# Eight groups of small steps set later in a one-core two-layer GDN and latent-attention kernel

## The reference, cut to what matters

```python
u = rms_norm(x, pre_mix)
qkv_a, z_a, a_a, b_a, cq, ckv, k_rope, gate_logits = split(u @ w_in)
qkv_a = silu(causal_conv(qkv_a, conv_w))          # width 4
q_a, k_a = l2_norm(q_a), l2_norm(k_a)             # per head of 128
g_a = -exp(A_log) * softplus(a_a + dt_bias); beta = sigmoid(b_a)
o_a = rms_norm(gated_delta_rule(q_a, k_a, v_a, g_a, beta)) * silu(z_a)
y_a = o_a @ w_branch_a
y_b = latent_attention(cq, ckv, k_rope) @ w_branch_b
x = x + rms_norm((sigmoid(g0) * y_a + sigmoid(g1) * y_b) @ w_out)
x = x + rms_norm(relu(rms_norm(x) @ w_ff1)**2 @ w_ff2)
```

## Time and profile before

| what | value |
|---|---|
| median of three runs | 1168.86 us (1162.62 to 1173.67) |
| the profiled execution | 1171.58 us |
| its span | 1169.8 us |
| TensorE matmuls busy | 1069.1 us, 91% |
| VectorE, ScalarE, GpSimd busy | 750.7, 568.7, 171.6 us |
| mean granted TensorE clock | 0.954 of full |

### The profile page before, as it was taken

One profiled execution on the slowest core, in us unless ns is written; L12 is line 12 of the kernel. 1 busy time (PEld: TensorE's weight loads), 2 busy tenths in 40 slices (PEclk: granted clock), 3 DMA queues, 4 the chain that ended last, 5 costly groups with the idle time before them and its releaser, 6 DMA issues.

```text
span 1169.8 us, 24158 instructions
## 1 busy us (share of the span) xinstructions
PE 1069.1 (91%) x10568; PEld 1033.3 (88%) x10568; DVE 750.7 (64%) x967; ACT 568.7 (49%) x789; POOL 171.6 (15%) x133
## 2 busy tenths in 40 slices
PE   6899878899999899999978988698899998999996
PEld 5888868789999899999878988697799997999996
DVE  6885526667757587744477845365786666886453
ACT  5565353663554444433356643545546444544431
POOL 7131000140000232200011300001400002221000
PEclk9989979998999899999979889799999998999999
DMA  7333322442455366566433433223423652665651
GB/s 256 106 121 105 115 70 90 125 132 88 145 179 182 108 185 194 169 207 184 144 108 108 145 97 107 69 94 110 145 88 129 216 185 88 217 185 191 185 182 49
DMA packets 45607, 163.84 MB, mean 140 GB/s; under 512 B 5184, under 2 KB 5440, under 8 KB 45504
## 3 DMA queue, kind: packets, MB, share of 16 engines
q1 hardware_dynamic: 44928, 161.50, 43.9%
q10 hardware_dynamic: 576, 0.81, 0.2%
HBM read 161.24 MB, written 1.05 MB: 139 GB/s over the span
## 4 chain that ended last, share of the span: by engine, by line
PE 76%; DVE 12%; ACT 6%; issue 4%; DMA 1%; SPq 0%; POOL 0%; POOLq 0%; DVEq 0%; ACTq 0%
PE dense L524 21%; PE dense L526 21%; PE dense L525 21%; DVE wlo L1235 4%; ACT whi L934 2%; DVE kT L1321 1%; PE sides L880 1%; PE sides L881 1%; DVE qT L1321 1%; PE sides L754 1%; PE sides L762 1%; DVE vT L1321 1%; PE sides L906 1%; ACT rn L945 1%; PE sides L916 1%
## 5 line engine op out<-in xcount | busy, mean ns | idle before, releaser
L1235 DVE TENSOR_TENSOR wlo<-raw,whi 128x1024 fp32r<-128x1024 f32 (+1 forms) x304 | 402.3, 1335 | 228.1 <-ACT whi L934 227.5
L934 ACT ACTIVATE whi<-raw 128x1024 fp32r<-128x1024 f32 (+1 forms) x304 | 314.1, 1046 | 216.9 <-PE dense L526 206.2
L524 PE MATMUL dense<-uh,whi 128*128 128x256 f32 x768 | 232.0, 302 | 3.4 <-DVE wlo L1235 2.0
L526 PE MATMUL dense<-uh,wlo 128*128 128x256 f32 x768 | 221.1, 288 | 2.7 <-issue 2.7
L525 PE MATMUL dense<-ul,whi 128*128 128x256 f32 x768 | 221.2, 288 | 1.1 <-issue 1.1
L524 PEld LDWEIGHTS dense<-uh,whi 128*128 128x128 f32 x768 | 151.8, 198 | 11.5 <-issue 7.6
L524 PE MATMUL dense<-fuh,whi 128*128 128x256 f32 x512 | 145.9, 285 | 9.8 <-DVE ful L1545 9.6
L525 PEld LDWEIGHTS dense<-ul,whi 128*128 128x128 f32 x768 | 151.7, 198 | 1.8 <-issue 1.4
L526 PEld LDWEIGHTS dense<-uh,wlo 128*128 128x128 f32 x768 | 151.4, 197 | 1.2 <-issue 1.2
L526 PE MATMUL dense<-fuh,wlo 128*128 128x256 f32 x512 | 145.2, 284 | 0.0
L525 PE MATMUL dense<-ful,whi 128*128 128x256 f32 x512 | 144.8, 283 | 0.0
(11 more groups left out here) (280 smaller groups left out, 2021.5 us busy)
## 6 DMA issues: line engine op xcount, KB each, us to landing
raw<-weights SPq DMA_DIRECT2D x304, 512.0 KB, 3.7
xT<-x_t SPq DMA_DIRECT2D x4, 256.0 KB, 4.4
out_t<-xT SPq DMA_DIRECT2D x4, 256.0 KB, 2.3
cst<-consts ACTq DMA_DIRECT2D x1, 512.0 KB, 7.0
prm_all<-params ACTq DMA_DIRECT2D x1, 150.0 KB, 3.9
pos_i<-pos ACTq DMA_DIRECT2D x1, 128.0 KB, 4.4
cst<-consts ACTq DMA_DIRECT2D x1, 2.0 KB, 4.8
```

Source lines behind the costliest of these rows:

```text
L524: mm(o_, h_[:, ws], ahi[:, k0 + k, :], start=is_first, stop=False, skip_group_check=True)
L526: x_ = mm(o_, l_[:, ws], ahi[:, k0 + k, :], start=False, stop=is_last, skip_group_check=True)
L934: return A(o_, i_, ACT.Copy)
L1235: TT(wlo[s][:, 0:w], raw[s][:, 0:w], f32(whi[s][:, 0:w]), ALU.subtract).then_inc(lo_ready, 1)
```

## The change

`schedule()` is rewritten between job `lat` 2 and job `uq` 0. Arithmetic, job order and weights are the same.

- `logits` becomes three steps: 0 behind job `k` 0 (PE's products and the first two operations of each of ScalarE and VectorE), 1 behind half `k` 1, 2 behind job `k` 1.
- All of `k` 1 to 3 and `z` 0 get halves; `gc` stands behind half `k` 2, `dt` 0 and 1 behind half `k` 3, `silu` n one half job later than before, `nrm`, `kk`, `dexp`, `ktrans`, `eg` spread over the halves of `z` 0 to 2; job `z` 3 is whole and stands ahead of `lvP` 0.
- `nrm` is split in `nsq` (GpSimd's squares, PE's sums) and `nrm` (ScalarE, VectorE), the second one later.
- The sixteen steps of the inverse and the state stand one each ahead of the sixteen halves of `v` and `q`; `vtrans` 0 to 3 behind job `v` 3, half `q` 0, half `q` 1 and job `q` 1; `silu` n of v and q one half job later.
- `kk` and `qk` go pair by pair of heads in the order 0, 2, 1, 3, so the first two need heads 0 to 3 only; `t_o` half 0 moves ahead of job `vt` 3, with the `side` banks swapped.
- The sign of `sinT` (GpSimd) becomes a step in the list behind `dt` 3.
- Layer 1 has the same three early splits as layer 0.
- SyncE issues the first quarter of x, then the first weight piece, then the other three quarters.

```diff
-    o += [("logits", 0), ("latn", 1)]
+    o.append(("latn", 1))
     job("k", 0)
-    o.append(("conv", 0))
+    o += [("logits", 0), ("conv", 0)]
+    half("k", 1)
+    o.append(("logits", 1))
     job("k", 1)
-    o += [("conv", 1), ("gc", 0), ("silu", 0), ("trig", 0), ("silu", 1)]
+    o += [("logits", 2), ("conv", 1)]
+    half("k", 2)
+    o += [("gc", 0), ("silu", 0), ("trig", 0)]
     job("k", 2)
-    o += [("conv", 2), ("dt", 0), ("dt", 1), ("silu", 2)]
+    o += [("silu", 1), ("conv", 2)]
+    half("k", 3)
+    o += [("dt", 0), ("dt", 1)]
     job("k", 3)
-    o += [("conv", 3), ("dt", 2), ("dt", 3), ("kr", 0), ("silu", 3), ("lnexp", 0)]
+    o += [("silu", 2), ("conv", 3), ("dt", 2), ("dt", 3), ("sign", 0), ("kr", 0)]
+    half("z", 0)
+    o += [("silu", 3), ("lnexp", 0), ("nsq", 0), ("nsq", 1), ("nrm", 0), ("nrm", 1)]
     job("z", 0)
...
+    between = [(kind, part, i) for kind in "vq" for i in range(4) for part in (half, job)]
+    behind = {n: [] for n in range(len(between) + 3)}
+    for n in range(8):
+        behind[2 * n + 2].append(("conv", 4 + n))
+        behind[2 * n + 3].append(("silu", 4 + n))
+    behind[0] += [("zsilu", i) for i in range(4)]
+    for n, at_ in enumerate((7, 8, 10, 11)):
+        behind[at_].append(("vtrans", n))
+    behind[15].append(("nsq", 4))
+    steps = [[(step, lv)] for lv in range(len(SIZES)) for step in ("lvP", "lvV")]
+    steps += [[(step, 0)] for step in ("pairP", "pairV", "lastP", "lastV")]
+    steps += [[(step, 0), (step, 1)] for step in ("t_v0", "t_st", "t_ks", "t_v1")]
+    for n, (kind, part, i) in enumerate(between):
+        o.extend(steps[n])
+        part(kind, i)
+        o.extend(behind[n])
+    half("gate", 0)
+    o += behind[16] + [("nsq", 5)]
     job("gate", 0)
-    o += [("lnexp", 1), ("nrm", 4), ("nrm", 5)]
+    o += behind[17] + [("lnexp", 1), ("nrm", 4), ("nrm", 5)]
     job("kn", 0)
+    o.append(("nsq", 6))
     job("kn", 1)
+    o.append(("nsq", 7))
+    job("kn", 2)
     o += [("nrm", 6), ("nrm", 7)]
-    job("kn", 2)
     job("kn", 3)
...
-            return {("xsplit", 1): 1, ("sq", 0): 2, ("sqsum", 1): 3}.get((what, n), 0) if l == 0 else 0
+            return l * NPIECE + {("xsplit", 1): 1 + l, ("sq", 0): 2 + l, ("sqsum", 1): 3 + l}.get((what, n), 0)
...
+            x_part(0)
             for n in range(DEPTH * NPIECE):
                 sp.wait_ge(lo_ready, n + 1)
                 sp.dma_start(raw[n % RING][:], w_in[n]).then_inc(loaded[n % RING], 16)
+                if n == 0:
+                    for c in range(1, 4):
+                        x_part(c)
```

More of the change, by code:

```diff
@@ L39 @@
 QUAD = 32
+PAIRS = [0, 2, 1, 3]
 KK_BANK = [4, 1, 3, 4]
+QK_BANK = [0, 2, 0, 2]
 SIZES = [2, 4, 8, 16]
@@ L138, in schedule @@
     job("z", 1)
-    o += [("kk", 0), ("kk", 1), ("dexp", 2), ("dexp", 3), ("eg", 0), ("eg", 1)]
+    o += [("kk", 2), ("ktrans", 0), ("eg", 0), ("eg", 1)]
     half("z", 2)
-    o += [("kk", 2), ("kk", 3), ("ktrans", 0), ("ktrans", 1), ("zero", 0)]
+    o += [("kk", 3), ("ktrans", 1), ("zero", 0)]
     job("z", 2)
     o.append(("x1", 0))
[L144 to L173, removed]
@@ L174, in schedule @@
-    for _ in fill:
-        pass
+    job("z", 3)
+    between = [(kind, part, i) for kind in "vq" for i in range(4) for part in (half, job)]
[8 more added lines that the diff above has]
+    steps = [[(step, lv)] for lv in range(len(SIZES)) for step in ("lvP", "lvV")]
@@ L187, in schedule @@
     job("vt", 2)
+    o.append(("t_o", 0))
     job("vt", 3)
-    o += [("t_o", 0), ("t_o", 1)]
+    o.append(("t_o", 1))
     for i in range(6):
@@ L480, in _, with x_part @@
         def _(sp):
-            for c in range(4):
+            def x_part(c):
                 sp.dma_start(xT[:, 2 * c:2 * c + 2, :], x_in[:, 2 * c:2 * c + 2, :]).then_inc(s_x[c], 16)
+            x_part(0)
             for n in range(DEPTH * NPIECE):
@@ L630, in norm, with logits @@
                 r.then_inc(sumsq, 1)
-            def logits(l, _):
+            def logits(l, part):
+                if part:
+                    return
                 pe.wait_ge(dve_evac, l * NDVE_EVAC + evacs_through(JOB["lat", 2])[1])
@@ L702, in ktrans @@
             def ktrans(l, half):
+                pe.wait_ge(nrm_out, due(l, nrm_out, 2 + 2 * half))
                 pe.wait_ge(kk_out, due(l, kk_out, 2 + half))
@@ L840, in t_o @@
             def t_o(l, half):
-                pe.wait_ge(qk_out, due(l, qk_out, 4))
-                pe.wait_ge(qd_out, due(l, qd_out, 2))
+                pe.wait_ge(qk_out, due(l, qk_out, 2 + 2 * half))
+                pe.wait_ge(qd_out, due(l, qd_out, half + 1))
+                if half == 0:
+                    pe.wait_ge(nrm_r, due(l, nrm_r, 15))
                 for e in range(4):
@@ L846, in t_o @@
                     cols = slice(e * P, (e + 1) * P)
-                    mm(side[half][:, cols], vn0[:, h, :], AT[:, half, e, :], start=True, stop=True)
-                    mm(side[2 + half][:, cols], st[:, h, :], qd[:, h, :], start=True, stop=False)
-                    r = mm(side[2 + half][:, cols], vn1[:, h, :], AT[:, 2 + half, e, :], start=False, stop=True)
+                    mm(side[1 - half][:, cols], vn0[:, h, :], AT[:, half, e, :], start=True, stop=True)
+                    mm(side[3 - half][:, cols], st[:, h, :], qd[:, h, :], start=True, stop=False)
+                    r = mm(side[3 - half][:, cols], vn1[:, h, :], AT[:, 2 + half, e, :], start=False, stop=True)
                 r.then_inc(t_om, 1)
@@ L918, in ysum @@
                 r.then_inc(y_mm, 1)
-            do = dict(norm=norm, logits=logits, dt=dt, job=job, gc=gc, vtrans=vtrans, nrm=nrm, latn=latn, kr=kr_, ktrans=ktrans, kk=kk, qk=qk,
+            do = dict(norm=norm, logits=logits, dt=dt, job=job, gc=gc, vtrans=vtrans, nsq=nsq, latn=latn, kr=kr_, ktrans=ktrans, kk=kk, qk=qk,
                       lvP=lvP, lvV=lvV, pairP=pairP, pairV=pairV, lastP=lastP, lastV=lastV, half=half, t_v0=t_v0, t_st=t_st, t_ks=t_ks, t_v1=t_v1, t_o=t_o, onrm=onrm,
@@ L999, in fsplit_x, with logits @@
                       scale=prm_all[:, l, PRE_FFN + c:PRE_FFN + c + 1]).then_inc(fu_hi, 1)
[L1001 to L1010, removed]
+            def logits(l, part):
+                if part == 0:
+                    act.wait_ge(ab_z, due(l, ab_z, 2))
+                    A(sm[:, 1, :], sm[:, 0, :], ACT.Abs).then_inc(ab_abs, 1)
+                    act.wait_ge(ab_abs, due(l, ab_abs, 1))
+                    A(sm[:, 2, :], sm[:, 1, :], ACT.Exp, scale=-1.0).then_inc(ab_ex, 1)
+                elif part == 1:
+                    act.wait_ge(ab_w, due(l, ab_w, 1))
+                    A(sm[:, 4, :], sm[:, 3, :], ACT.Ln).then_inc(ab_ln, 1)
+                else:
+                    act.wait_ge(ab_sp, due(l, ab_sp, 3))
+                    A(sm[:, 8, :].rearrange("p (t n) -> p t n", t=NT)[:, :, 8:16],
+                      sm[:, 7, :].rearrange("p (t n) -> p t n", t=NT)[:, :, 8:16], ACT.Exp, scale=-1.0).then_inc(ab_a, 1)
             def job(l, j):
@@ L1152, in t_o @@
                 act.wait_ge(t_om, due(l, t_om, half + 1))
-                copy(oT[:, hs, 0:P], side[half][:])
-                copy(oT[:, hs, P:2 * P], side[2 + half][:]).then_inc(t_oo, 1)
+                copy(oT[:, hs, 0:P], side[1 - half][:])
+                copy(oT[:, hs, P:2 * P], side[3 - half][:]).then_inc(t_oo, 1)
             def onrm(l, i):
@@ new lines, in logits @@
+                if part == 0:
+                    dve.wait_ge(ab_mm, due(l, ab_mm, 1))
+                    raw_ = side[2][:, 0:32].rearrange("p (t n) -> p t n", t=NT)
+                    TT(by_t(0)[:, :, 0:8], raw_[:, :, 0:8], over_t(prm_all[:, l, DTB:DTB + H]), ALU.add).then_inc(ab_z, 1)
+                    TS(by_t(0)[:, :, 8:16], raw_[:, :, 8:16], -1.0, None, ALU.mult).then_inc(ab_z, 1)
+                elif part == 1:
+                    dve.wait_ge(ab_ex, due(l, ab_ex, 1))
+                    TS(sm[:, 3, :], sm[:, 2, :], 1.0, None, ALU.add).then_inc(ab_w, 1)
+                    dve.wait_ge(ab_w, due(l, ab_w, 1))
+                    STT(sm[:, 5, :], sm[:, 3, :], -1.0, sm[:, 2, :], ALU.add, ALU.subtract).then_inc(ab_w, 1)
+                    V.reciprocal(sm[:, 6, :], sm[:, 3, :]).then_inc(ab_rc, 1)
+                    dve.wait_ge(ab_w, due(l, ab_w, 2))
+                    dve.wait_ge(ab_rc, due(l, ab_rc, 1))
+                    TT(sm[:, 5, :], sm[:, 5, :], sm[:, 6, :], ALU.mult).then_inc(ab_sp, 1)
+                else:
+                    dve.wait_ge(ab_sp, due(l, ab_sp, 1))
+                    dve.wait_ge(ab_ln, due(l, ab_ln, 1))
+                    TT(sm[:, 7, :], sm[:, 4, :], sm[:, 5, :], ALU.subtract).then_inc(ab_sp, 1)
+                    dve.wait_ge(ab_sp, due(l, ab_sp, 2))
+                    STT(sm[:, 7, :], sm[:, 0, :], 0.0, sm[:, 7, :], ALU.max, ALU.add).then_inc(ab_sp, 1)
+                    dve.wait_ge(ab_sp, due(l, ab_sp, 3))
+                    dve.wait_ge(ab_a, due(l, ab_a, 1))
```

(8 more changed lines are left out.)

53 lines of the change are left out of this document (28 added, 25 removed).

## The result

The changed kernel takes 1122.6 us (median of four, 1113.2 to 1125.4) against 1165.7 before (four runs now, 1161.4 to 1173.7); the ratio is 0.9608, 95% interval 0.9528 to 0.9689. The forecast was 1123. The medians are 43.1 us apart. The profiled execution's span went from 1169.8 to 1120.4 us, 49.4 less.

A forecast was written before the change was run, and what follows sets the result against it. TensorE sets the end, so its waits and lower-clock time can be won. 30.9 + 8.1 + 7.1 - 2.0 + 2.5 + 0.4 = 47.0 us off 1171.6 gives 1124.6, as median 1123 us; range 1107 to 1142.

The forecast's parts named there:

- Part 1: `vtrans`: 22.4 us of waits go, 2.7 new ones come, 11.2 return from the clock; 30.9 us gained (14 to 34).
- Part 2: First step of the inverse: the wait for `x1` and one lower-clock stretch go in each layer; 8.1 us (5 to 9).
- Part 3: l2 norms and `qk`: waits of 4.8 and 2.3 us go; 7.1 us gained (5 to 7.5).
- Part 4: Logits, `gc`, `dt`: the logits' wait moves, `gc` newly waits 2.3 and 4.0 us; -2.0 us (-9 to +7).
- Part 5: Start of layer 1: a piece split ahead of `xsplit` 1 brings the first `wlo` earlier; 2.5 us (1 to 4).
- Part 6: First load: first piece lands earlier but constants wait for x's second quarter; 0.4 us gained (-1 to 2).
- The clock: Lower-clock terms inside the parts: 11.2 (`vtrans`), 3.0 (inverse), 1.5 (around 69 to 76 us) gained; 3.0 lost at `gc`.
- Rival A: The clock does not follow: idle time goes but as many lower-clock stretches stay; 1139 us, chance 0.17.
- Rival B: No wait moves: VectorE's list is shorter than walked, `gc` and `t_v0` find their input; 1111 us, chance 0.17.
- C: TensorE waits for ScalarE's turn at each of the 32 inverse and state steps; 1186 us, chance 0.03.
- D: Another producer holds `vtrans`, so its long wait stays; only 16 us come through, 1153 us, chance 0.08.
- my 0: GpSimd's sign step moved behind `dt`: taken to cost 0, at most 2.1 us lost, once.

The follow-up runs named there:

- the experiment: Job `z` 3 cut again, its second piece behind `lvP` 0, against the changed kernel: ratio 0.9660 to the kernel before, 1128.0 us.
- the yardstick: The changed kernel itself, unedited, run again for comparison with the edits: ratio 0.9592 to the kernel before, 1119.9 us.
- the second logits run: Repeat of the changed kernel with the three logits steps ahead of `latn` 1 again: ratio 0.9519 to the kernel before, mean 1109.9 us.
- the best version: Changed kernel with early logits, half `gate` 2 ahead of `sc` 0, and constants' load waiting for x's first quarter: ratio 0.9421 to the kernel before, mean 1098.5 us.

## Why the prediction was right

The total was right, and so were the mechanism and most terms: 47.0 us were forecast from the profile, 49.4 came between the profiles and 43.1 between the medians. That the median lies within 0.4 us of the forecast is luck, as runs of one kernel lie 12 us and more apart.

- Part 1, forecast 30.9: 28.3 us between `v` 0 and `gate` 0 in the two layers, or 30.0 with the sums of `nsq` 4, which now stand in this stretch (0.9 us a layer). `vtrans` went; the new wait at `t_v0` is 1.18 us in each, forecast 1.3, from the walk through ScalarE's list. Undoing both edits of this part cost 29.

```profile
165.92 0.46 PE L823 MATMUL sides<-vtok,XT 128*128 128x128 f32 x2 [1.18 <-ACT vtok L945]
```

- Part 2, forecast 8.1: 11.4 in the table (4.3 and 7.1), 8.1 in the stretch of the experiment and 7.9 by its whole time. One lower stretch in each layer was forecast; the experiment brought it in layer 1 alone.
- Part 3, forecast 7.1: 8.1 in the table, and 6.3 without `nsq` 4. A wait of 0.5 at `nsq` 6 in each layer was not forecast.
- Part 4, forecast -2.0: -2.2 (1.05 and -3.25). That this is so near is luck too: by the yardstick's profile the same stretch gives +1.5, and the seven profiles with this code, 6 us apart, have a mean of 131.6, while the code before took 130.4 and (in the `vtrans` edit of the kernel before) 127.7. So the loss is 1 to 4 us. The wait moved from `logits` to `latn` 1: 3.84 and 1.83 us. Waits of 2.3 and 4.0 at `gc` were forecast; 1.06 and 3.10 came.

```profile
38.64 2.93 PE L701 MATMUL sides<-sq_q,cst 128*128 128x256 f32 x6 [3.84 <-DVE rl L1357]
...
55.34 0.38 PE L650 MATMUL sides<-sm,cst 128*128 128x32 f32 x2 [1.06 <-ACT sm L1023]
```

  In part 4 VectorE's list was walked well: `ab_g` came 16.6 us behind L1357's end, 16.9 forecast. The term that was mis-sized is TensorE's way there, 15.7 us instead of 14.6 in layer 0 and 13.7 instead of 12.9 in layer 1; in layer 0 the piece behind `latn` 1, at the lower clock for most of its length, took 4.3 us and not 3.3. Undoing the logits' move alone gave 7 us, more than my 2. In the sum I had set against the logits' cost what `dt` and `wlo` gain; that a part of this gain comes from the other moves of that stretch, and so stays when the logits go back, would explain the difference, but no run took it apart.
- Part 5, forecast 2.5: 3.3. Part 6, forecast 0.4: 0.7 at the first product, 0.3 at the second job.
- The clock: 11.2 + 3.0 + 1.5 - 3.0 = 12.7 were forecast inside the parts; 14 is all that isn't idle time, 4.5 in dense matmuls and 9.4 in light ones. Rival A, 1139, is out by the time, and by the lower clock's 66.4 us instead of 107.4. In layer 0 the stretches of lower clock about 40 and 72 us are still there, and the one at `gc` of layer 1 (606.8 to 613.7 us) is new; the yardstick's profile has none at either `gc`, where I had set one each.

Rival B (no wait moves) is out by the rows at L650 and L701, C because TensorE waits for no other engine from `lvP` to `pairV`, D by `vtrans`, which is gone. Two slips in the rivals' sums changed nothing: parts 2, 3 and 5 make 17.7 us and not 16, and 32 steps at 1.5 make 48 and not 49.

The sign step of GpSimd took 1.09 us, beside conv 3. It set the squares behind it later, and a `wlo` beside them took 2.06 us; in layer 1, which has no sign step, that `wlo` took 1.21. `dt` 3 waits 1.1 us in layer 0, before 1.6, and not at all in layer 1; in the yardstick's profile it waits 0.7 in layer 1 and not in layer 0.

```profile
64.31 1.09 POOL L1629 TENSOR_SCALAR sinT<-sinT,cst 128x256 f32<-128x256 f32 x1
65.37 2.32 POOL L1612 TENSOR_TENSOR sq<-kT 128x512 f32<-128x512 f32 x2
...
66.71 2.06 DVE L1250 TENSOR_TENSOR wlo<-raw,whi 128x1024 fp32r<-128x1024 f32 x1
```

So my 0 may be up to 0.8 us too good. By the rule of the Trainium skill that the prediction names ("SBUF — State Buffer", section "Who interferes with whom") it could have been 2.1, and these rows agree with the rule in kind, not in that size; no experiment took it apart.

## What to carry to other kernels

Where each engine works through one hand-written list, look not for the engine that waits but for the first thing in the releasing engine's list that it can't do yet: 22 us of TensorE's waits were for a copy that stood behind a `silu` behind a conv. Setting `silu` one half job later and the four copies one to a step took all but 2.4 us of it away, and neither edit alone did. Ask of each wait removed what stands next in the list and who gives it: the logits' wait was for the same row of operations that `latn` 1 needs. Where the releasing engine's list is itself what ends last in a stretch, as VectorE's was from `lat` 2 to `dt`, reordering mostly carries the wait to another line: three orders of the same steps left 52.5 to 54.3 us of idle time in all. Less work there is what I would try next; no run here tried it. And put independent work ahead of a wait: one line, `half("gate", 2)`, took 5.6 us of wait for the rotary part away and moved none of it. And read small effects from a stretch of the profile: the `vtrans` order alone cost 6.4 us there, and 1.6 in the whole time.

## What the hardware showed that was not expected

Matmul pace changed within full granted clock. In the profile of the kernel without the early splits, two stretches of the FFN, TensorE busy throughout, clock 1.00 in both:

```profile
400.00:440.00 40.00, 40.00 (x356) 40.00 (x355) 34.48 (x31) 19.77 (x23) 10.90 (x8) 1.00 0.65 209
940.00:980.00 40.00, 40.00 (x342) 40.00 (x341) 35.00 (x33) 20.97 (x24) 11.35 (x8) 1.00 0.67 209
```

That is 356 matmuls against 342 in 40 us: one every 0.113 us instead of 0.118 from start to start, 4% quicker. It held for some 1500 matmuls from 390 to 545 us (about 7 us won), began and ended at no event of the program that I can name, and appeared in one layer's FFN in four of the 14 profiles (also in those of the cut `z` 3, the second logits run and the best version), in none of the three of the changed kernel. Its cause is open. The 7 us are about half of the spread between runs of one kernel (1107.6 to 1123.2 us for five of the changed one on one chip), and that spread is why effects of 2 or 3 us were read from local rows and not from totals. I take it as the likely source of a part of that spread; a run's time was not tied to it.

Idle time also cost more than itself: with both `vtrans` edits undone, `v` 0 to `uq` 0 had 16.9 us more idle time and took 31.1 us longer, 47.8 us of it at the lower clock instead of 6.8.
